# Expert slots kept by token tile: 32 for each of two tiles instead of 56 for both, and a gather over three PSUM banks

## What is computed

```python
def moe_ffn(x, router_w, router_b, w_gate, w_up, w_down, s_gate, s_up, s_down):
    scores = jax.nn.sigmoid((x @ router_w).astype(jnp.float32))
    ...
    _, idx = lax.top_k(masked, TOP_K)                 # 8 of 64, from 4 of 8 groups
    gate = gate / jnp.sum(gate, -1, keepdims=True) * ROUTED_SCALE
    ...
        hb = jax.nn.silu(xb @ w_gate[e]) * (xb @ w_up[e])
        return y.at[tok].add((hb @ w_down[e]) * wt[:, None]), None
    ...
    return y + shared
```

## Time and profile before

| | us |
|---|---|
| median of 3 runs | 1337.0 (1336.21 to 1337.35) |
| profiled execution, span | 1335.2 |
| TensorE busy | 1302.7 |
| VectorE busy | 420.9 |
| ScalarE busy | 304.5 |
| DMA, mean over the span | 335 GB/s |
| L408, gather matmuls, high and low parts of x | 102.4 and 93.3 |
| L395, up products | 450.5 |
| L457, down products | 226.5 |
| L449, combine, high and low parts | 113.8 and 101.4 |

### The profile page before, as it was taken

The page is one execution under the profiler, slowest core; times in us unless marked ns, Lnnn a source line. Parts: engine busy times, 40 slices in busy tenths (PEclk is TensorE's granted clock), DMA queues, the critical chain, the costliest instruction groups (busy, mean ns, idle before and its releaser), DMA issues.

```text
span 1335.2 us, 15678 instructions
## 1 busy us (share of the span) xinstructions
PE 1302.7 (98%) x6220; PEld 654.2 (49%) x6220; DVE 420.9 (32%) x903; ACT 304.5 (23%) x661; POOL 28.1 (2%) x101
## 2 busy tenths in 40 slices
PE   8999999999999999999989999999999999999996
PEld 5777754344443434444346565444434343444432
DVE  4576364212121221212143556321212112121213
ACT  3354331111111111111122343112111111121112
POOL 1013000000000000000000000000000000000000
PEclk9999989999999999999999998999999999999998
DMA  9314067889999999999982619578999999999991
GB/s 365 140 72 190 1 259 292 321 334 431 420 436 418 426 419 423 427 417 439 425 315 107 252 64 359 236 305 352 432 424 423 425 425 435 415 436 424 428 417 73
DMA packets 34221, 447.27 MB, mean 335 GB/s; under 512 B 4996, under 2 KB 6404, under 8 KB 16004
## 3 DMA queue, kind: packets, MB, share of 16 engines
q1 hardware_dynamic: 33648, 446.28, 80.4%
q10 hardware_dynamic: 532, 0.43, 0.1%
HBM read 445.65 MB, written 1.05 MB: 335 GB/s over the span
## 4 chain that ended last, share of the span: by engine, by line
PE 95%; DVE 3%; ACT 1%; issue 0%; DMA 0%; DVEq 0%; SPq 0%; ACTq 0%
PE psum L395 33%; PE psum L457 17%; PE psum L449 10%; PE psum L408 9%; PE psum L2027 4%; PE psum L2169 4%; PE psum L1142 3%; PE psum L1590 2%; PE psum L549 2%; PE psum L434 1%; PE psum L1428 1%; PE psum L2175 1%; PE psum L1187 1%; PE psum L582 1%; PE psum L1208 1%; PE psum L441 1%
## 5 line engine op out<-in xcount | busy, mean ns | idle before, releaser
L395 PE MATMUL psum<-w_up_ring,moe_x_selected 128*64 128x512 f32 x2048 | 450.5, 592 | 0.0
L395 PEld LDWEIGHTS psum<-w_up_ring,moe_x_selected 128*64 128x64 f32 x2048 | 146.8, 137 | 290.4 <-issue 290.4
L457 PE MATMUL psum<-w_down_ring,moe_hT 128*64 128x512 f32 x992 | 226.5, 598 | 0.0
L992 DVE SCALAR_TENSOR_TENSOR moe_h<-moe_silu,moe_slot_gate,psum 128x256 f32<-128x256 f32 x64 | 30.8, 481 | 381.3 <-ACT moe_silu L759 381.3
L457 PEld LDWEIGHTS psum<-w_down_ring,moe_hT 128*64 128x64 f32 x992 | 65.7, 136 | 128.5 <-issue 128.3
L997 DVE TENSOR_TENSOR moe_out_low<-psum,moe_out_high 128x512 fp32r<-128x512 f32 x64 | 44.3, 692 | 233.1 <-ACT moe_out_high L771 233.1
L759 ACT ACTIVATE moe_silu<-psum 128x256 f32<-128x256 f32 x64 | 24.6, 385 | 405.9 <-PE psum L395 405.9
L449 PE MATMUL psum<-moe_out_high,moe_matchT 128*128 128x512 f32 x256 | 113.8, 444 | 1.4 <-DVE moe_out_low L999 1.4
L408 PE MATMUL psum<-moe_match,moe_x_high 128*128 128x448 f32 x256 | 102.4, 400 | 0.0
L449 PE MATMUL psum<-moe_out_low,moe_matchT 128*128 128x512 f32 x256 | 101.4, 396 | 0.0
L408 PE MATMUL psum<-moe_match,moe_x_low 128*128 128x448 f32 x256 | 93.3, 364 | 0.0
(11 more groups left out here) (494 smaller groups left out, 1113.9 us busy)
## 6 DMA issues: line engine op xcount, KB each, us to landing
w_up_ring<-in_moe_up SPq DMA_DIRECT2D x60, 4096.0 KB, 15.7
w_down_ring<-in_moe_down SPq DMA_DIRECT2D x62, 2048.0 KB, 13.6
w_up_ring<-in_moe_up SPq DMA_DIRECT2D x8, 2048.0 KB, 12.4
w_up_ring<-in_ev_columns SPq DMA_DIRECT2D x4, 2048.0 KB, 15.7
w_up_ring<-in_od_w_in SPq DMA_DIRECT2D x4, 2048.0 KB, 13.1
w_up_ring<-in_ev_out SPq DMA_DIRECT2D x2, 2048.0 KB, 7.7
moe_shared_weights<-in_shared_up SPq DMA_DIRECT2D x2, 2048.0 KB, 7.8
moe_w_down_extra<-in_moe_down SPq DMA_DIRECT2D x2, 2048.0 KB, 18.0
```

Source lines behind the costliest of these rows:

```text
L395: last = nc.tensor.matmul(k.psum[e * SLOTS:(e + 1) * SLOTS, 6, :], xsel[:, kk, own:own + SLOTS], up_view(slots[e], kk), start=kk == 0, sto ...
L457: last = nc.tensor.matmul(k.psum[e * SLOTS:(e + 1) * SLOTS, bank, :], hT[:, j * P + e * SLOTS:j * P + (e + 1) * SLOTS], places[e][:, j, ha ...
```

## The change

Slots are kept by tile. A token's place is its number among the expert's tokens of its own tile, and each expert has 32 slots for each tile, 64 together and all used. A tile's tokens only go to that tile's slots, so a gather matmul has 8 x 32 = 256 columns, and the two tiles write two halves of the bank. The number of gather matmuls stays 32. Row groups go over banks 4, 5 and 7 in turn, so TensorE waits for the copy of the group three before. The evicted groups have 512 columns, not 448. To make bank 7 free, `pe_turn` writes bank 6, except for the first two pairs.

The transposed match matrix is made for four pairs at once and the same for both tiles; ACT copies it out twice, each time scaled by `own_tile`, which is 1 in the slots of a tile and 0 in the others. Match matrices on DVE have half the elements in fewer instructions. The places need one matmul instead of three, the counts one instead of two. Two constants are added on POOL, and the clearing of unused slots goes.

```diff
-CAPACITY = 56
+CAPACITY = 32
+SLOTS = NT * CAPACITY
...
+    gather_bank = (4, 5, 7, 4, 5, 7, 4, 5)
...
+        pe_wait(s.match, matched)
         for kk in range(KD):
-            if kk >= 2:
-                nc.tensor.wait_ge((s.xsel_a, s.xsel_b)[kk % 2], taken + kk // 2)
+            if kk >= 3:
+                pe_wait((s.xsel_a, s.xsel_b)[(kk - 3) % 2], taken + (kk - 3) // 2 + 1)
             for t in range(NT):
...
+                cols = slice(t * 8 * CAPACITY, (t + 1) * 8 * CAPACITY)
                 for part in (x_high, x_low):
-                    last = nc.tensor.matmul(k.psum[:, 4 + kk % 2, 0:8 * CAPACITY], part[:, t, kk, :], match[:, t, :, 0:CAPACITY],
-                                            start=t == 0 and part is x_high, stop=t == NT - 1 and part is x_low)
+                    last = nc.tensor.matmul(k.psum[:, gather_bank[kk], cols], part[:, t, kk, :],
+                                            match[:, t].rearrange("p e s -> p (e s)"), start=part is x_high, stop=part is x_low)
...
-    def pe_turn_match(pairs):
...
+    def pe_turn_match(pairs=4):
+
+        for i in range(pairs):
+            last = nc.tensor.matmul(k.psum[:, 5, i * P:(i + 1) * P], match_bf[:, 2 * i:2 * i + 2].rearrange("p e t s -> p (e t s)"),
+                                    k.ident_bf[:], start=True, stop=True)
         return last
...
-                last = nc.tensor.matmul(k.psum[:, 2 * t + half, :], matchT[:, i, t * P:(t + 1) * P],
+                last = nc.tensor.matmul(k.psum[:, 2 * t + half, :], matchT[:, t, i, :],
...
+                pe.wait_ge(s.xsel_b, 4 * q + 7)
                 pe_slot_gates().then_inc(s.slot_gates, 1)
-            pe_combine((i - 1) % 4, 0)
-            if i < 2:
-                pe_turn_match((2 * i, 2 * i + 1)).then_inc(s.match_turned, 1)
-            pe.wait_ge(s.h, p + 1)
-            if i == 3 and not final:
-                pe.wait_ge(s.gates_read, q + 2)
-            pe_turn().then_inc(s.turned, 1)
+                pe.wait_ge(s.h, p + 1)
+                pe_turn().then_inc(s.turned, 1)
+                pe_combine(2, 0)
+            else:
+                pe_combine((i - 1) % 4, 0)
+                pe.wait_ge(s.h, p + 1)
+                pe_turn().then_inc(s.turned, 1)
             pe_combine((i - 1) % 4, 1).then_inc(s.combined, 1)
+            if i == 0:
+                pe_turn_match().then_inc(s.match_turned, 1)
...
             if i == 3 and not final:
                 pe.wait_ge(s.xsel_a, 4 * q + 8)
+                pe.wait_ge(s.gates_read, q + 2)
...
+        def take_match(q):
+            act.wait_ge(s.match_turned, q + 1)
+            for t in range(NT):
+                last = nc.scalar.activation(matchT[:, t].rearrange("p i n -> p (i n)"), k.psum[:, 5, :], ACT.Copy,
+                                            scale=k.own_tile[:, t:t + 1])
+            last.then_inc(s.matchT, 1)
```

More of the change, by code:

```diff
@@ L360, in output_and_experts @@
     shT = sb("shared_hT", [P, NT, KF, P])
-    count = sb("expert_tokens", [MAX_OVER, N_EXP])
-    c1 = sb("over_64", [MAX_OVER, N_EXP])
-    c2 = sb("over_128", [MAX_OVER, N_EXP])
+    count = sb("expert_tokens", [MAX_OVER, NT, N_EXP])
+    over1 = sb("over_32", [MAX_OVER, NT, N_EXP])
+    over2 = sb("over_64", [MAX_OVER, NT, N_EXP])
+    c1 = sb("extra", [MAX_OVER, N_EXP])
+    c2 = sb("earlier_expert", [MAX_OVER, N_EXP])
     c3 = sb("extra_before", [MAX_OVER, N_EXP])
@@ L415, in pe_gather_two, with two_filled, two_gathered @@
             for t in range(NT):
+                cols = slice(c * P + t * 2 * CAPACITY, c * P + (t + 1) * 2 * CAPACITY)
                 for part in (x_high, x_low):
-                    last = nc.tensor.matmul(k.psum[:, bank, c * P:(c + 1) * P], part[:, t, 4 * (bank - 4) + c, :],
-                                            match[:, t, 0:2, :].rearrange("p e s -> p (e s)"),
-                                            start=t == 0 and part is x_high, stop=t == NT - 1 and part is x_low)
-        return last
+                    last = nc.tensor.matmul(k.psum[:, bank, cols], part[:, t, 4 * (bank - 4) + c, :],
+                                            match[:, t, 0:2, :].rearrange("p e s -> p (e s)"), start=part is x_high,
+                                            stop=part is x_low)
+        return last
+    def two_filled(first):
+        return [xsel[:, first:first + 4, 0:P].rearrange("p c (e t s) -> p c t e s", e=2, t=NT)[:, :, t] for t in range(NT)]
+    def two_gathered(bank):
+        return [k.psum[:, bank, :].rearrange("p (c t e s) -> p c t e s", c=4, t=NT, e=2)[:, :, t] for t in range(NT)]
     def pe_slot_gates(pairs=4):
@@ L813, in scalar @@
                 act.wait_ge(s.gather_a, i + 4 * QUADS + 1)
-                nc.scalar.copy(xsel[:, 0:4, 0:P], k.psum[:, 4, :].rearrange("p (c n) -> p c n", c=4)).then_inc(s.xsel_a, 1)
+                for to, of in zip(two_filled(0), two_gathered(4)):
+                    last = nc.scalar.copy(to, of)
+                last.then_inc(s.xsel_a, 1)
                 act.wait_ge(s.up, i + PAIRS + 1)
```

169 lines of the change are left out of this document (77 added, 92 removed).

## The result

The changed kernel takes **1313.4 us**, median of 4 runs (1313.0 to 1315.1), against 1337.0 before. The ratio is 0.983, with a 95% interval from 0.981 to 0.984: faster by 23.6 us where 27.8 were forecast. The time lies inside the range given, 4.2 us above the predicted one. The profiled execution has a span of 1311.7 us where the one before had 1335.2, so the two profiles differ by 23.5 us and explain the whole of it.

A forecast was written before the change was run, and what follows sets the result against it. TensorE set the pace before; afterwards DMA binds some turns into each layer (58.25 us a turn against TensorE's 55.7). Lead, gaps and slack give 14.6 + 13.2 = 27.8 us: 1337.0 - 27.8 = 1309.2 us, range 1304 to 1317.

The forecast's parts named there:

- Two resources full at once: In the loop before the change, TensorE needs 59.10 us a turn of four pairs and the DMA 58.25.
- rival C: No DMA limit in the loop, queues could go faster: all 50 us of TensorE saved, 1287 us; chance 0.03.
- The gather, 3.2 us less, and a turn of 55.7: Loop gather, 14 times: 7.23 to 4.05 us at 0.125 a step; TensorE's turn falls from 59.10 to 55.7 us.
- rival A: Weight load sets the gather step at 0.19 us: 1.2 us saved a gather, 1315 us; chance 0.08.
- The first gather, 1.0 us, idle of 2: First gather, twice: TensorE keeps 1.0 of 3.2 us (bounds 0 to 1.8), idling about 2 before the slot gates.
- lead: Pair 6's weights asked for earlier in each layer: 1.0 + 0.2 + 0.2 + 3.2 = 4.6 us.
- DMA gaps closed: 25 landings, pair 6 to 31, take 364 us at 432 GB/s: 7.4 us less in layer 0, 5.5 in layer 1.
- slack used up: Each layer's last weights arrived 2.7 and 3.2 us before use; less 0.1 to start, 2.6 and 3.1 us gained.
- The waits: TensorE waits for weights before up products from about pair 15: up to 1.8 us at pair 3, 0.8 at pair 2.
- Rival B: Clock falls to 0.50 after new idle: first gather 1313 to 1316 us, in the loop up to 1330; chance 0.13.
- DMA at 424: Rival D: loop's mean DMA rate stays 424 GB/s, the second part falls away, 1322 us; chance 0.06.
- overflow: Rival E: extra-pass loop runs if an expert has over 32 tokens in a tile: 1341 or 1373 us; chance 0.02.

The follow-up runs named there:

- the one execution told of above: Profiled execution, 1309.1 us, of the changed kernel with pair 4's down weights asked before pair 3's and the third down-weight place refilled for pair 24; median 1307.4 us.
- the run with pair 12: Changed kernel with first gate products behind first up products, pair 4's down weights before pair 3's, third down-weight place refilled for pair 12: 1304.3 us.
- the run with the old order: Same edits as the run with pair 12, but pair 3's down weights asked for before pair 4's again: 1305.9 us.
- the reordered ones: Changed kernel with pair 4's down weights before pair 3's, third place refilled: 1307.4 us; with early first up product 1304.4 (pair 24), 1304.3 (pair 12).

## Why the prediction was right, and what was off by 4 us

**Two resources full at once.** Right. The pair of runs with fewer weights shows it from both sides, and the rival C, no limit by DMA, is at 1287.0 us with the limit taken away, where it was forecast at 1287.

**The gather, 3.2 us less, and a turn of 55.7.** Right: 7.23 to 4.10 us is 3.13, with 4.05 forecast, and TensorE's own turn is 55.73 us. The step was taken as 0.125 us from the slope between 448 and 512 columns and is 0.12. The rival A (0.19 a step, by the length of a weight load) is out: the profile's rows still give the loads 0.19, and they pass every 0.12. On this the Trainium skill ("TensorE: Matmul & The Clock Gate", section "Wait — 56ns, not 53.3ns?") gives columns / 2.4 GHz and 2.5 ns more from start to start, which is 109 ns for 256 columns. The trace has 119, and 205 for 448 columns where the rule gives 189, so here it is 10 to 16 ns short a step. By it the gather would be 0.3 us shorter, which in the second half of a layer nobody would see.

**The third bank.** Right that no wait over 0.1 us is left. What the prediction didn't price is the gather without it: 1.6 us more.

**The first gather, 1.0 us, idle of 2.** From its first matmul to the slot gates it takes 6.65 us and not 7.75, so 1.1 us less in either layer, and the idle time ahead of the slot gates is 1.70 us. The first up product starts 0.86 us earlier in layer 0, whose gather started 0.3 later in this execution. In layer 1 the stretch from the end of layer 0 to the first up product is 1.25 us shorter (153.84 against 155.09).

**The sum, term by term.** For each layer, from the landings above and the earlier trace rows, in us:

| | forecast 0 / 1 | measured 0 / 1 |
|---|---|---|
| lead: pair 6's weights land earlier | 4.6 / 4.6 | 3.9 / 4.4 |
| DMA gaps closed: 25 landings less | 7.4 / 5.5 | 5.2 / 4.2 |
| slack used up | 2.6 / 3.1 | 2.6 / 3.1 |
| together | 14.6 / 13.2 | 11.7 / 11.7 |

(Pair 6's counterpart in layer 1 lands 932.7 - 916.6 = 16.1 us earlier; 11.7 of that come from layer 0.)

The second term was mis-sized. The prediction let 25 landings take 25 x 14.56 = 364 us, by the 432 GB/s of the best stretch. They take 366.2 and 365.3. The steady pace is 14.61 us a pair (pair 15's up product at 429.32, pair 31's at 663.06: 233.74 / 16), which is 430.7 GB/s, and makes 25 steps 1.2 us a layer longer. That is all of it in layer 1; in layer 0 another 1.0 goes in the first steps, where the queues are still short of places (404 GB/s from 285 to 300 us, below). 431 and 432 GB/s look alike on the page, and over 50 steps they are 2.4 us. Nor was 432 the top of the loop, as the prediction says: two of the 40 slices of the page before, 33 us each, have 436 and 439. The slices of that loop go from 417 to 439, so one stretch is a rough measure of the pace. The pace could have been read from the packets of the kernel before: half of them take no more than 1.213 us at 32 KB (up weights) and 0.611 at 16 KB (down), and with 128 of each a pair over 16 DMA engines, 8 x (1.213 + 0.611) gives an estimate of 14.59 us a pair.

```profile
285.00:300.00 15.00, 15.00 (x72) 6.15 (x72) 2.16 (x4) 3.57 (x7) 0.00 (x0) 1.00 0.98 404
```

The lead was short by 0.7 in layer 0, where the up weights of pair 6 were asked for 4.2 us earlier, not 4.6, and took 0.3 longer from issue to landing. In layer 1 they were asked for 16.3 us earlier (903.0 against 919.3), which is 4.6 beside layer 0's 11.7, and took 0.2 longer. Together the two terms lack 4.4 us, which is the whole miss.

**The waits.** Expected from about pair 15 on, none in turns 1 and 2: so it is. Expected up to 1.8 us at pair 3 of a turn and 0.8 at pair 2: they are 1.56 to 1.66 at pair 3 of every turn from pair 15 on, and 0.69 at pair 26.

**The clock.** In the profiled execution the granted clock is 1.00 through both expert stages, the 1.7 and the 1.6 us of idle time included. It is 0.50 from 684.6 to 691.4, behind 3.09 us of idle time between the layers, as before. Rival B did not come about here. But its mechanism is real: in the one execution told of above the same idle time ahead of the slot gates was followed by a clock of 0.50, and the cost was 1.7 us, half of the 3.4 that the prediction priced, since the stretch was half as long. Its other half, falls at the waits in the loop, I found in no trace.

**DMA at 424, and overflow.** The mean rate over the loop rose from 424 to 430 GB/s with the shorter gather, so D is out, and the 424 was gaps, not a limit. No matmul of the overflow branch is in the trace. On the rate the Trainium skill ("DMA: Bandwidth & Descriptors", section "Where 436 GB/s comes from") again names 358 and 435; the loop holds 430 for 378 us, so by this trace the first doesn't bind.

## What to carry to other kernels

When a stretch shows two resources at a share of 1.00, work out the second one's time for a turn before pricing an edit to the first: here 50 us of TensorE work were worth 23.6, and then 26 us of TensorE work could be added back for 5. The term to get right is then the second resource's steady pace, to half a per cent, from the first use to the last over as many turns as there are, or from the time of its packets; the rate of one good window was too good. And once the stream binds, what counts is what lets it start and keeps it fed: 2 us off the head of a layer and a buffer place used twice gave 9 us without a matmul less.

## What the runs showed of the hardware

- Waits cost more than the profile's idle column says: 21.6 us of waits in it, 26.5 us of time when their cause was taken away, about a quarter of a us more for each of 18 waits.
- The same 1.7 us of idle time ahead of the same matmuls stands ten times in the profiled executions (two layers of five kernels); nine times the granted clock stayed at 1.00, once it was 0.50 for 3.4 us behind it.
- In the trace the up product mostly starts 0.5 to 0.6 us after the end of the last packet of its weights where it waits for them, twice 1.7 us (pair 51 of the run with pair 12, pair 30 of the run with the old order), so that much of a landing is not on the queues' record.
- Weight loads of 128 columns, 0.19 us each in the rows, pass one every 0.12 us beside matmuls of 256 columns, so the 0.19 is not the step from one to the next.
- A stream of loads can be on time with its first packets and late with its last: at the same rate, the 128 packets of a 4096 KB load stretched over 11.4 to 11.8 us late in the layers of the changed kernel and over up to 14.2 in the reordered ones.
